# A two-block hybrid layer on one core: square-root norms, a gate tile between convolution and decays, block inverses in half the transfers, and reordered router, combine and second-block steps

## The reference, cut to what matters

```
proj = rms_norm(x, norm1_w) @ w_in                       # 256 x 1024 @ 1024 x 6752
c = silu(centred_dwconv(conv_in, conv_w, conv_b))        # 7 taps, 4608 channels
q, k, v, xs, Bm, Cm = split(c)
q = l2_normalize(q) * 128 ** -0.5 ; k = l2_normalize(k)  # 8 heads of 128: t * rsqrt(sum(t * t) + EPS)
o_gdn = gated_delta(q, k, v) forward + backward          # A = strict(beta * (k k^T) * decay); unit triangular solve per chunk
y     = ssd(xs, dt, A, Bm, Cm) forward + backward        # 16 heads of 64
h = x + concat(rms_norm(o_gdn) * silu(g_gate), rms_norm(y * silu(z))) @ w_out
aff = softmax(rms_norm(h, norm2_w) @ w_router)           # 16 experts
vals, idx = top_k(aff^T, 32)                             # each expert takes 32 tokens
h = h + scatter(silu(xs @ w_gate) * (xs @ w_up) @ w_down * vals)
x = rms_norm(h, final_norm_w)
```

## Time and profile before

| | |
|---|---|
| median of 3 runs | 1417.66 us (1416.61 to 1420.83) |
| the profiled execution's own time | 1422.65 us |
| its span | 1420.8 us |
| mean granted TensorE clock | 0.954 |
| busy TensorE / VectorE / ScalarE / GpSimd | 88% / 46% / 29% / 23% |
| chain that ended last | 61% TensorE, 13% DMA, 11% VectorE, 7% ScalarE, 5% GpSimd |

### The profile page before, as it was taken

One profiled execution on the slowest core, in us unless ns is written; L12 is line 12 of the kernel. 1 busy time (PEld: TensorE's weight loads), 2 busy tenths in 40 slices (PEclk: granted clock), 3 DMA queues, 4 the chain that ended last, 5 costly groups with the idle time before them and its releaser, 6 DMA issues.

```text
span 1420.8 us, 17974 instructions
## 1 busy us (share of the span) xinstructions
PE 1246.5 (88%) x7458; PEld 943.0 (66%) x7458; DVE 652.0 (46%) x1045; ACT 406.0 (29%) x975; POOL 329.9 (23%) x321
## 2 busy tenths in 40 slices
PE   6989689899889699978786999998878999899977
PEld 5878555477654442212126899898778889898867
DVE  1597748133460310001015355575786346567764
ACT  4345532133530220100004531321423451220431
POOL 0486621412300100000020212233253012223240
PEclk9999889999999699999997999999999999999998
DMA  5324223766307679999990435334332245335210
GB/s 187 128 110 157 80 89 126 259 237 226 130 1 295 231 289 420 422 421 422 421 359 1 164 118 182 119 128 169 119 107 83 75 171 179 129 114 182 91 60 30
DMA packets 90515, 256.97 MB, mean 181 GB/s; under 512 B 6605, under 2 KB 11494, under 8 KB 78018
## 3 DMA queue, kind: packets, MB, share of 16 engines
q1 hardware_dynamic: 88082, 248.61, 46.2%
q0 software_dynamic: 2032, 6.95, 1.6%
q10 hardware_dynamic: 320, 0.26, 0.1%
HBM read 253.42 MB, written 2.12 MB: 180 GB/s over the span
## 4 chain that ended last, share of the span: by engine, by line
PE 61%; DMA 13%; DVE 11%; ACT 7%; POOL 5%; issue 2%; SPq 1%; DVEq 0%; ACTq 0%; POOLq 0%
PE bank L680 57%; DMA ring<-in_w_up_dram 8%; DMA ring<-in_w_down_dram 4%; PE bank L689 4%; DVE ring_r L1905 3%; POOL late L2481 3%; POOL acc L2482 2%; DVE acc L1976 2%; ACT xT L1461 1%; DMA ring<-in_w_ada_dram 1%; ACT ring L1461 1%; ACT cT L1461 1%; ACT L1461 1%; ACT oa L1461 1%; ACT qkT L1461 0%
## 5 line engine op out<-in xcount | busy, mean ns | idle before, releaser
L2584 POOL CAST w_hi_r<-ring 128x1024 fp32r<-128x1024 f32 x136 | 152.3, 1148 | 691.3 <-DMA ring<-in_w_in_dram 273.1
L680 PE MATMUL bank<-ring_r,xT_hi 128*128 128x256 f32 (+1 forms) x864 | 247.9, 287 | 0.0
L1905 DVE TENSOR_TENSOR ring_r<-ring,w_hi_r 128x1024 fp32r<-128x1024 f32 x136 | 188.1, 1414 | 68.6 <-POOL w_hi_r L2584 68.6
L680 PE MATMUL bank<-w_hi_r,xT_hi 128*128 128x256 f32 x704 | 209.0, 297 | 6.5 <-DVE xT_r L1910 4.4
L680 PE MATMUL bank<-w_hi_r,xT_r 128*128 128x256 f32 x704 | 202.9, 288 | 0.0
L680 PEld LDWEIGHTS bank<-ring_r,xT_hi 128*128 128x128 f32 x864 | 170.4, 197 | 0.2
L680 PEld LDWEIGHTS bank<-w_hi_r,xT_hi 128*128 128x128 f32 x704 | 138.0, 196 | 19.6 <-issue 10.3
L680 PEld LDWEIGHTS bank<-w_hi_r,xT_r 128*128 128x128 f32 x704 | 137.3, 195 | 0.0
L680 PE MATMUL bank<-ring,xsT 128*32 128x512 f32 x496 | 111.6, 595 | 24.9 <-DMA ring<-in_w_up_dram 12.8
L680 PE MATMUL bank<-xT,ring 128*128 128x256 f32 x576 | 127.6, 384 | 0.0
L680 PEld LDWEIGHTS bank<-xT,ring 128*128 128x128 f32 x576 | 110.9, 193 | 15.4
(11 more groups left out here) (353 smaller groups left out, 2124.9 us busy)
## 6 DMA issues: line engine op xcount, KB each, us to landing
ring<-in_w_in_dram SPq DMA_DIRECT2D x39, 2048.0 KB, 7.6
ring<-in_w_up_dram SPq DMA_DIRECT2D x32, 1024.0 KB, 16.3
ring<-in_w_down_dram SPq DMA_DIRECT2D x32, 1024.0 KB, 16.4
ring<-in_w_gate_dram SPq DMA_DIRECT2D x30, 1024.0 KB, 16.3
ring<-in_w_ada_dram SPq DMA_DIRECT2D x12, 2048.0 KB, 8.9
ring<-in_w_out_dram SPq DMA_DIRECT2D x8, 2048.0 KB, 8.1
ring<-in_w_o_mla_dram SPq DMA_DIRECT2D x2, 2048.0 KB, 12.4
ring<-in_w_o_swa_dram SPq DMA_DIRECT2D x2, 2048.0 KB, 7.7
```

Source lines behind the costliest of these rows:

```text
L680: return release(nc.tensor.matmul(o, lhsT, rhs, start=start, stop=stop))
L1905: tt(lo, raw_, hi.bitcast(F32), ALU.subtract).then_inc(lo_done.sem, lo_done.one("piece"))
L2584: nc.gpsimd.tensor_copy(hi, raw_).then_inc(hi_done.sem, hi_done.one("piece"))
```

## The change

It joins many edits:

- The convolution's norms: ScalarE takes a square root (one pass of eight 128x512), and VectorE takes the reciprocal in place ahead of `normed`. The second four come behind tile 29 and not 32 on VectorE, and behind tile 24 and not 26 on ScalarE.
- `kq_decay` has four pairs of banks. The first gate tile (n = 0, t = 0) is computed ahead of the decays, the second one behind them and behind four transposes.
- The 16x16 blocks go out in 4 transfers and not 8; of the 8 transfers that bring the inverses back, 4 are issued by ScalarE.
- The modulation: blocks 0 and 1 ahead of the first turn, then 3, 3, 2 and 2 blocks in the turns (`ADA`).
- `ssd_args(0)` one step earlier, other banks for it; the state-space norm by ln and exp.
- Router: the residual is transposed without the norm, its first half inside the output projection; logits are summed in four strips of 32 rows and added up by a matmul with `same`; the norm's scale comes in with the exponential. The normed tokens are written by ScalarE and their low part by GpSimd. `selw` comes behind `sel`; the last four of the eight gather steps follow the first expert block.
- Combine: the final norm is done for each token tile by itself, interleaved with the combine and the next norm; tables are loaded ahead (`warm`).
- Second block: `first_jobs` starts when half of a tile's split is there; on VectorE the low parts of the gates' weights, `token_out(0)` of the third branch and the low parts of `w_out_2` stand elsewhere.

```diff
...
+        ADA = [(2, 3, 4), (5, 6, 7), (8, 9, None), (10, 11, None)]
...
+            def gate_tile(n, t, w):
+                if n == 0:
+                    pe.wait_ge(*((norm_act.sem, 8) if t == 0 else (lt_dve.sem, lt_dve.at("qkd", 7))))
+                elif n == 1:
+                    pe.wait_ge(e_act.sem, e_act.at("E", 6 + t))
+                else:
+                    pe.wait_ge(gate_act.sem, 2 * (n - 2) + t + 1)
+                    if n == 2 and t == 0:
+                        pe.wait_ge(lt_dve.sem, lt_dve.at("qkd", 6))
+                for k in range(DK):
+                    last = mm(bank[4 + 2 * (n % 2) + t][:], xT[:, k, t * P:(t + 1) * P], w[:, k, :], k == 0, k == DK - 1)
+                last.then_inc(gate_pe.sem, 1)
...
+                    pe.wait_ge(conv_in.sem, CT - 2)
...
+                elif h == 1:
+                    pe.wait_ge(conv_in.sem, CT)
+                elif h == 2:
+                    pe.wait_ge(gate_act.sem, 1)
+                if h >= 4:
+                    pe.wait_ge(lt_dve.sem, lt_dve.at("qkd", h - 4))
...
+            first_gate = take("w_in")
+            gate_tile(0, 0, first_gate)
             for h in range(GH):
                 kq_decay(h)
-            gate_block(0)
+            for i in range(4):
+                nat_bank(i)
+            gate_tile(0, 1, first_gate)
+            block_read()
             gate_block(1)
-            for i in range(9):
+            for i in range(4, 9):
...
+            for n in range(ADA[0][0]):
+                ada_rows(n, 0)
+                if n:
+                    ada_cols(n - 1)
+            pe.wait_ge(gate_act.sem, 8)
+            pe.wait_ge(nat_out.sem, 13)
             pe.wait_ge(lt_pool.sem, GH)
             for r in range(GH // 2):
-                ada_rows(3 * r, r)
+                n0, n1_, n2_ = ADA[r]
+                if r == 0:
+                    ada_cols(n0 - 1)
+                ada_rows(n0, r)
...
+            def token_transposes(half):
+                for t in range(TT):
+                    pe.wait_ge(out_dve.sem, 2 * half + t + 1)
+                    for b in (2 * half, 2 * half + 1):
+                        for j in range(2):
+                            k = 2 * b + j
+                            last = tr(q4(bank[b], 2 * j + t), xres[:, t, k * P:(k + 1) * P])
+                        if t:
+                            last.then_inc(rt_pe.sem, rt_pe.one(f"x{b}"))
+            def logit_sums(half):
+                for j in range(4):
+                    k = 4 * half + j
+                    if half and j % 2 == 0:
+                        pe.wait_ge(*((rt_act.sem, rt_act.at("n2")) if j == 0 else (rt_dve.sem, rt_dve.at("n3"))))
+                    last = mm(bank[5][32 * j:32 * j + 32, 0:T], w_r[:, k, :], xT[:, k, :], half == 0, half == 1)
+                return last
...
+                        if k8 and half and t:
+                            token_transposes(0)
...
+            pe.wait_ge(load_router, 64)
+            pe.wait_ge(rt_act.sem, rt_act.at("n1"))
+            logit_sums(0)
+            token_transposes(1)
+            logit_sums(1).then_inc(rt_pe.sem, rt_pe.one("sums"))
+            pe.wait_ge(rt_dve.sem, rt_dve.at("sums"))
             for t in range(TT):
-                for k in range(DK):
-                    last = mm(bank[4][:, t * NE:(t + 1) * NE], xT[:, k, t * P:(t + 1) * P], w_r[:, k, :], k == 0, k == DK - 1)
+                last = mm(bank[4][:, t * NE:(t + 1) * NE], work[:, t * P:(t + 1) * P], same)
             last.then_inc(rt_pe.sem, rt_pe.one("logits"))
...
+                            if gi == pair == o == k0 == 0:
+                                gather(4)
...
-                pe.wait_ge(xs_dve.sem, xs_dve.at(f"x{2 * t + 1}", l))
+                pe.wait_ge(xs_dve.sem, xs_dve.at(f"x{2 * t}", l))
...
-            def inverse_norms(i0):
+            def norms(i0):
 
                 for i in range(i0, i0 + 4):
                     act.wait_ge(norm_pe.sem, i + 1)
                     n = GD if i < 4 else 1
-                    last = f(nsq[i], bank[4 + i % 4][:], ACT.Ln, scale=float(n), bias=EPS * n)
-                link(last)
-                for i in range(i0, i0 + 4):
-                    f(nsq[i], nsq[i], ACT.Exp, scale=-0.5).then_inc(norm_act.sem, 1)
+                    f(nsq[i], bank[4 + i % 4][:], ACT.Sqrt, scale=float(n), bias=EPS * n).then_inc(norm_act.sem, 1)
...
-                if n in (18, 26):
-                    inverse_norms(n // 2 - 9)
+                if n in (18, 24):
+                    norms(0 if n == 18 else 4)
...
+            act.wait_ge(inv_out, 16)
+            for q in range(QN):
+                act.dma_start(Xc[q * SQ:(q + 1) * SQ, :, :, 1, :].rearrange("p h c n -> p (h c) n"), block_rows(inverses, 1, q)
+                              ).then_inc(inv_back, 16)
...
+            def high_part(t):
+                f(xn2[:, t, :], xres[:, t, :], ACT.Copy, scale=small[:, 6 + t:7 + t])
+                f(xn2_hi[:, t, :], xres[:, t, :], ACT.Copy, scale=small[:, 6 + t:7 + t]).then_inc(rt_act.sem, rt_act.one(f"hi{t}"))
             act.wait_ge(rt_dve.sem, rt_dve.at("max"))
-            f(aff[:], aff[:], ACT.Exp).then_inc(rt_act.sem, rt_act.one("exp"))
+            for t in range(TT):
+                last = f(aff[:, t, :], aff[:, t, :], ACT.Exp, scale=small[:, 6 + t:7 + t], accum_out=stat[:, 2 + t:3 + t])
+            last.then_inc(rt_act.sem, rt_act.one("exp"))
+            high_part(0)
+            high_part(1)
...
+                inverse(nsq[i])
...
-                if n in (24, 32):
-                    for i in range(n // 2 - 12, n // 2 - 8):
+                if n in (24, 29):
+                    for i in range(0 if n == 24 else 4, 4 if n == 24 else 8):
...
+            combine(0)
             split_lo(0)
-            dve.wait_ge(cmb_act.sem, 1)
-            inverse(small[:, 2:4])
+            combine(1)
+            combine(2)
             dve.wait_ge(load_moe, 16 * N_MOE)
-            dve.wait_ge(cmb_dve.sem, cmb_dve.at("h1"))
-            for t in range(TT):
-                stt(out=xres[:, t, :], in0=xres[:, t, :], scalar=small[:, 2 + t:3 + t], in1=f_norm[:], op0=ALU.mult,
-                    op1=ALU.mult).then_inc(cmb_dve.sem, cmb_dve.one(f"done{t}"))
+            final_norm(0)
+            combine(3)
...
+            normed_tokens(0, 0)
+            final_norm(1)
+            split_tokens(0, 0)
...
-                        split_lo(read + 1)
+                        split_lo(read - 1)
...
+                        if b and it == 0:
+                            split_lo(read + 1)
...
+                        if it == (UNITS if b == 2 else UNITS - 1):
...
-                        if i == 2:
-                            split_lo(read + (3 if b == 2 else 2))
+                        if i == (1 if b == 2 else 2):
+                            split_lo(read + 2)
...
-            for d in range(2):
-                for q in range(QN):
-                    pool.dma_start(block_rows(blocks, d, q),
-                                   LT[q * SQ:(q + 1) * SQ].rearrange("p h (c d) n -> p (h c) d n", c=TT)[:, :, d, q * SQ:(q + 1) * SQ]
-                                   ).then_inc(blocks_out, 16)
-            pool.wait_ge(blocks_out, 16 * 2 * QN)
+            for q in range(QN):
+                both = bass.AP(tensor=blocks.tensor, offset=q * 32 * SQ * SQ, ap=[[SQ, SQ], [SQ * SQ, 2 * GH * TT], [1, SQ]])
+                pool.dma_start(both, LT[q * SQ:(q + 1) * SQ].rearrange("p h i n -> p (h i) n")[:, :, q * SQ:(q + 1) * SQ]
+                               ).then_inc(blocks_out, 16)
+            pool.wait_ge(blocks_out, 16 * QN)
             for d, dst in ((0, Uin), (1, Uraw)):
-                pool.dma_start(dst[64 * d:64 * d + 64, :], blocks[64 * d:64 * d + 64, :]).then_inc(blocks_in, 16)
+                one = bass.AP(tensor=blocks.tensor, offset=d * SQ * SQ, ap=[[2 * SQ * SQ, 64], [1, SQ * SQ]])
+                pool.dma_start(dst[64 * d:64 * d + 64, :], one).then_inc(blocks_in, 16)
...
```

360 lines of the change are left out of this document (207 added, 153 removed).

## The result

The changed kernel takes 1403.1 us (median of 4 runs, 1401.6 to 1405.7), the kernel before 1419.2 us beside it. The ratio is 0.989, with a 95% interval of 0.986 to 0.992: 1.1% faster, where 0.8% was forecast. Its profiled execution has a span of 1401.5 us, 19.3 less than before.

| stretch of the program | predicted | measured |
|---|---|---|
| start to the gates' end (norms, gate tile, banks) | +13.9 | -0.8 (260.1, was 260.9) |
| modulation, gates' end to the delta rule's end | +6.4 | +7.5 |
| state-space stage | -1 | +1.0 |
| output projection | 0 | +0.8 |
| router, from the projection's end through the experts | -11.2 | -7.9 |

What follows compares the result with a forecast made beforehand. TensorE, busy 88% of the span, was taken as the bound. Terms 20.3 - 1 - 11.2 - 9.5 - 10 = -11.4 took the profiled 1422.65 us to 1411.3, on the median's scale 1406; range 1383 to 1421.

Steps and rivals of the forecast that it cites:

- From above: 0.15 + 511 x 7.3 ns = 3.9 us: Convolution norms: upper estimate for one 128x512 reciprocal on VectorE, extended from the small reciprocals' slope; taken for all eight, 31 us.
- a hole of 7.8 closes: VectorE at the convolution's end: idle time that goes as ScalarE's second norms move, so taps end 23.4 later, at 205.5.
- rival of dear reciprocals: Convolution norms: reciprocals stretch beside GpSimd's work; slower than 1421.9 from 5.9 us each, 1427 at 6.5; chance 0.16.
- the sign: Front: TensorE's first decay head would follow an idle stretch of over 10 us although the gate tile is done.
- Without the reciprocals it would have been 17 earlier: Front: the gates' end without reciprocals on VectorE, 17 earlier, where the forecast with them had 274.8, 13.9 later than 260.9.
- 4.1 gained: Router: half the gather behind the first expert block leaves 6.3 of 10.4 us ahead of the experts.
- it goes through the experts undiminished: Expert stage: the router's 11.2 us gain survives whole, since the experts end a fixed time after the first slot is free.
- the router's gain stays in the stream: Rival, experts: if the ring is not full, the weight stream and not the first block sets their end; 1417, chance 0.10.
- 750.1: Combine to second block: time near which TensorE was to start the second block, 9.5 earlier.
- 1.1 lost at each of four places: Second block: cost of putting the gate parts' low pieces behind the first maxima, gate sums ending at 896.2 where 895.09 was.
- 3 us or at a half clock 5: Second block: duration of the gate sums on TensorE after two low pieces are ready at about 893.2.
- The forecast's case: Whole kernel: the forecast with its terms moving within their bounds, 1392 to 1413; chance 0.53.

## Why the prediction came out as it did

**Norms.** The mechanism was right: the reciprocals stand on the path to the decays, and taking them away brought 22 of their 27 us. Two sizes were off. "From above: 0.15 + 511 x 7.3 ns = 3.9 us" measured 3.35, which is 6.3 ns for each element behind the first; eight times that is 4.4 us less. And I took the taps' duration as fixed. In the changed kernel 54 taps take 28.2 us, and before they took 32.8 (7.09, 11.30, 3.91 and 10.54); the step that failed is "a hole of 7.8 closes" as the only saving. So the taps ended 11.6 later and not 23.4, of which 4.4 and 4.6 are these two; the rest is a first norm 1.05 sooner, a second hole of 0.49 that closes too, and products that overlap with the reciprocals. The rival of dear reciprocals rested on GpSimd stretching them; it doesn't, 3.35 us beside it and without it. It does go with longer taps, and it has 8 of the 36 tiles and VectorE 28 (48 and 168 multiply-adds in the trace), not 9 and 27.

**Gate tile and banks.** The taps' end to the last `qkd` product: 16.6 predicted (its parts add up to 16.8), 207.87 - 193.75 = 14.1 measured. The idle stretch ahead of the first decay head was 8.68 us, where over 10 was named as the sign. The gates then took 52.2 us (52.7 predicted). "Without the reciprocals it would have been 17 earlier" measured 20.6 (240.3 against 260.9).

**Modulation.** 6.4 predicted, 7.5 measured, with the mechanism as stated; undoing it gave 11, or 9 without the state-space stage's part. The wait for the second block's load was 6.99, 8 predicted; what I had left out is a third one of 2.23 for the next block's load.

**State-space stage.** A gain of 1 predicted, a loss of 1 measured. I looked at ScalarE's exponentials only and not at TensorE's clock. Where the clock came back early behind the long wait, the predicted gain was there (37.4 to 37.6 us against 38.4).

**Router.** "4.1 gained" for the gather was wrong, and with it "it goes through the experts undiminished". In the changed kernel the second expert block is read at about 517, 19.6 behind the gather's start, where it had been 17.4. The stream restarts when slots are read: the next four loads (shown above) are issued over 9.72 us from 509.15 on, and were over 4.24 from 513.97 on, so that the last of them goes out at nearly the same time, 518.9 and 518.2. The second half of the gather stands ahead of that second read in either order. Without this term the prediction would have said 7.1, and 7.9 was measured. This is the rival "the router's gain stays in the stream" for a third of the gain. The four passes on ScalarE cost the 3.1 stated (485.47 to 489.62, of which the transposes hide one), but moving them alone makes the ranks ready only 0.4 sooner beyond the earlier start, since what VectorE loses beside GpSimd takes the rest back.

**Combine.** 9.5 predicted, 9.6 measured, counted from the combine's start. The first product stands at 750.68, near the 750.1 written down, which is chance: the 750.1 counts on the combine's old start, 730.92, and it happens to start at 731.63 now. Which of the combine's edits won it no run shows; nor was the router's first half (transposes without the norm) or the transfers undone alone.

**Second block.** Right in sum (10.4) and wrong in its parts. The moves of `token_out` and of the low parts of `w_out_2` were worth more than I took: 7.8 and 6.2 us in the second block (7.8 and 7.1 by the medians), where the text has 6.4 and 5. The half splits and the tables (3 predicted) were not undone by themselves. The low parts behind the maxima cost more too: "1.1 lost at each of four places" measured 3.9, 3.2, 3.2 and 3.9 at the second unit's scores, and still 2.6, 1.9, 0.3 and 1.7 at the third's, 6.5 in all where 4.4 was reckoned. The two pieces were there nearly when I said (5.6 us behind the scores' start, 5.2 reckoned; with the text's own 2 and 3.16 it would have been 6.0). The step that failed is "3 us or at a half clock 5", where I went on with the 3: behind a wait of 4.9 us the gate sums and what follows took 5.4, at a granted clock of 0.50 throughout. And the prediction priced only the order it had: half the pieces ahead would have won 24.5 us more.

**The sum.** The front came out 13.6 better than stated, and the state-space stage, the projection and the router together 6.1 worse; the combine and the second block add 0.5 to the good. That leaves 8 us on the span. On the median it is 3 (1406.3 forecast, 1403.1 measured): the profiled execution of before, 1422.65, lies 5.0 above the median of 1417.66 that the forecast started from, and that of the changed kernel, 1403.5, only 0.4 above its own. The forecast's case held, with 1403 inside its own range of 1392 to 1413, but that it came so close is partly luck: the first line of the table was off by 14.7 us, the stages behind it by 6 the other way, and the place of the two profiled executions against their medians took off 4.6 of the remaining 8.

## What to carry to other kernels

Where an edit takes work off one engine and puts it on another, price it on the receiving engine at full width, and ask what that engine's neighbour does at that moment: the same VectorE instruction took 0.50 or 0.65 us, and a scan 0.68 or 2.71, with what GpSimd did beside it, while the reciprocals and the maxima took the same time either way. When two orders of a block of work each leave a wait, look for the cut between them; half the pieces ahead and half behind removed both. And an edit that is measured only together with others can hide a loss: three parts of this change, each undone alone, made the kernel 11 to 22 us faster.

## What was not expected of the hardware

A reciprocal of 128x512 costs 3.35 us on VectorE, where the small ones' slope gave 3.9. The Trainium skill, page "VectorE: DVE Perf Modes", section "First, the fixed hardware budget", calls it an iterated divide with a repeat count of 8, from which I had estimated 4.3; the trace shows 4.9 times the product's 0.69 and not 8 times.

A scan over 16x256 slowed fourfold beside one GpSimd subtraction, while the maxima and replacements ahead of it (0.42 and 0.40 each) did not slow at all, though a like subtraction ran beside several of them too. Behind a wait of 7.26 or 7.27 us TensorE's clock came back to 1.00 after 3.5 us in one kernel and after 9.4 in another.
